# Wider moving operands in the feed-forward units: two activation halves in 512 columns, and 512 weight columns per token-major product

## The reference

```python
x = x + jnp.square(jax.nn.relu(h2 @ w_up)) @ w_down          # layer one, D_FF = 4096
...
# two more layers, each with two gated feed-forwards of width 2816:
# (silu(h @ gate) * (h @ up)) @ w_down, RMS norms before and after
```

## Time and profile before

| what | value |
|---|---|
| median of 3 runs | 1453.48 us (1450.79 to 1454.17) |
| profiled execution, its own time | 1449.68 us |
| its span | 1447.9 us |
| TensorE busy | 1393.1 us, 96% |
| VectorE busy | 915.3 us, 63% |
| ScalarE busy | 723.5 us, 50% |
| GpSimd busy | 192.2 us, 13% |

### The profile page before, as it was taken

The page is one execution under the profiler, slowest core; times in us unless marked ns, Lnnn a source line. Parts: engine busy times, 40 slices in busy tenths (PEclk is TensorE's granted clock), DMA queues, the critical chain, the costliest instruction groups (busy, mean ns, idle before and its releaser), DMA issues.

```text
span 1447.9 us, 28167 instructions
## 1 busy us (share of the span) xinstructions
PE 1393.1 (96%) x11538; PEld 1350.0 (93%) x11538; DVE 915.3 (63%) x1317; ACT 723.5 (50%) x1149; POOL 192.2 (13%) x210
## 2 busy tenths in 40 slices
PE   5889899999999999999999999999999998999998
PEld 5777789999999999998899999999999987999998
DVE  7998776666545655547766565556565467656554
ACT  7722745544434544446447444445454474544443
POOL 0465000022100111004201111011110010111100
PEclk9999899999999999999999999999999999999999
DMA  9233324555554545553434555544555441355551
GB/s 372 102 115 108 139 88 141 186 198 176 202 185 172 198 176 213 179 202 135 158 120 148 189 186 194 199 175 175 185 207 181 169 173 59 120 190 185 194 199 59
DMA packets 36814, 244.33 MB, mean 169 GB/s; under 512 B 4208, under 2 KB 5360, under 8 KB 8816
## 3 DMA queue, kind: packets, MB, share of 16 engines
q1 hardware_dynamic: 34992, 238.17, 45.4%
q10 hardware_dynamic: 1728, 4.81, 0.9%
HBM read 241.67 MB, written 1.05 MB: 168 GB/s over the span
## 4 chain that ended last, share of the span: by engine, by line
PE 84%; DVE 9%; ACT 4%; issue 2%; DMA 1%; DVEq 0%; ACTq 0%
PE ps L1906 50%; PE ps L1948 27%; DVE wlo L1094 3%; PE ps L2144 1%; PE ps L2170 1%; ACT whi L599 1%; PE ps L2160 1%; ACT ahi L853 1%; ACT pP L789 1%; PE ps L1964 1%; PE ps L2049 1%; DVE zz L1279 1%; DVE pP L1385 0%; DVE t L1241 0%; DVE t L1240 0%
## 5 line engine op out<-in xcount | busy, mean ns | idle before, releaser
L1094 DVE TENSOR_TENSOR wlo<-raw,whi 128x1024 fp32r<-128x1024 f32 (+1 forms) x434 | 505.7, 1207 | 256.2 <-ACT whi L599 256.0
L1906 PE MATMUL ps<-ahi,whi 128*128 128x256 f32 x2112 | 598.9, 284 | 21.8 <-DVE wlo L1094 17.5
L599 ACT ACTIVATE whi<-raw 128x1024 fp32r<-128x1024 f32 (+1 forms) x434 | 427.7, 1034 | 348.5 <-PE ps L1948 178.9
L1906 PE MATMUL ps<-alo,whi 128*128 128x256 f32 x2112 | 591.9, 280 | 0.0
L1906 PE MATMUL ps<-ahi,wlo 128*128 128x256 f32 x2112 | 591.1, 280 | 0.0
L1906 PEld LDWEIGHTS ps<-ahi,whi 128*128 128x128 f32 x2112 | 398.6, 189 | 29.1 <-DVE wlo L1094 13.0
L1906 PEld LDWEIGHTS ps<-alo,whi 128*128 128x128 f32 x2112 | 397.9, 188 | 0.7 <-issue 0.7
L1906 PEld LDWEIGHTS ps<-ahi,wlo 128*128 128x128 f32 x2112 | 398.1, 189 | 0.0
L1842 POOL TENSOR_TENSOR hlo<-fh,hhi 128x256 f32 (+3 forms) x104 | 85.8, 825 | 747.4 <-ACT hhi L909 534.5
L1550 DVE TENSOR_TENSOR fa<-ps,r 128x512 f32<-128x512 f32 x104 | 72.0, 692 | 173.8 <-PE ps L1906 173.6
L1948 PE MATMUL ps<-whi,hhi 128*128 128x256 f32 x960 | 149.5, 276 | 0.0
(11 more groups left out here) (350 smaller groups left out, 1346.8 us busy)
## 6 DMA issues: line engine op xcount, KB each, us to landing
raw<-in_w_gu SPq DMA_DIRECT2D x88, 1024.0 KB, 4.8
raw<-in_w_fd SPq DMA_DIRECT2D x44, 1024.0 KB, 4.8
raw<-in_w_up SPq DMA_DIRECT2D x16, 1024.0 KB, 4.8
raw<-in_w_dn SPq DMA_DIRECT2D x16, 1024.0 KB, 4.8
raw<-in_w_ret SPq DMA_DIRECT2D x13, 1024.0 KB, 4.8
raw<-in_w_mg SPq DMA_DIRECT2D x8, 1024.0 KB, 4.9
raw<-in_w_o SPq DMA_DIRECT2D x8, 1024.0 KB, 5.8
raw<-in_w_mem SPq DMA_DIRECT2D x4, 1024.0 KB, 4.8
```

The source lines that it names most:

```text
L599: nc.scalar.activation(whi[:, m % SPL, c], raw[:, n % RAW, c], ACT.Copy).then_inc(S("w_hi"), 1)
L1094: ins = tt(wlo[:, m % SPL, c], raw[:, n % RAW, c], whi[:, m % SPL, c].bitcast(F32), ALU.subtract)
L1906: ins = mm(dst, lhsT, rhs, start=k == 0 and p == 0, stop=k == kt - 1 and p == len(pairs) - 1)
```

## The change

The first pass gets a PE routine of its own, `ffn_unit`. `ahi` and `alo` become two halves of one tile `act2`, and one matmul moves both against `whi` (512 columns, the high products into the left half of a bank, the low ones into the right half); a second matmul of 256 columns adds `wlo` times high to the left half. Each column block now has a bank of its own (banks 0 or 1 and 4 or 5). ACT copies the right half to a new tile `fl`, DVE adds it to the left half and then scales by `r`, once for each column block. ACT's and DVE's orders within a unit change with it. In `down` each stationary block is used against two chunks of 512 weight columns. `hhi` and `hlo` now begin at a multiple of 128 bytes, as the weights do. PE waits ahead of the second token tile of the first down unit, because bank 4 or 5 still holds the last unit's sums. Some semaphores are merged.

```diff
-        w[0] += (64 - w[0]) % 128
+        w[0] += -w[0] % 128
         hhi = sb("hhi", [P, FF1_T, T], F32R, where=w)
...
+        def ffn_banks(g):
+
+            return two(g % 2), two(4 + g % 2)
...
# ScalarE
+                def low_sum(i, u, c):
+                    if c:
+                        sem, v = done(up + u)
+                        act.wait_ge(sem, at_round(v, i, RAW))
+                    else:
+                        act.wait_ge(S("ffn_left"), at_round(h0 + u + 1, i, RAW))
+                    nc.scalar.activation(fl[:, u % 2, c], ffn_banks(g0 + u)[c][:, 1], ACT.Copy).then_inc(S("low_sum"), 1)
...
                 def hidden(i, u):
+                    opening = i is None and u == 0
...
+                        low_sum(i, u, 0)
+                        high(i, u - 1)
+                        weights(up + u, i, UNIT)
+                    if kind == "gu":
+                        act.wait_ge(S("joined"), at_round(3 * (h0 + u) + 2, i, 3 * RAW))
+                        nc.scalar.activation(fs[:, b], fa[:, b, 0:T], ACT.Silu).then_inc(S("silu"), 1)
+                    if not opening:
+                        low_sum(i, u, 1)
...
# VectorE
-                    tt(fab, two((g0 + u) % 2), over(r[:, 0:T], 2), ALU.mult).then_inc(S("evac"), 1)
-                    if i is not None or u:
-                        weights(up + u, i, UNIT)
+                    for c, bank in enumerate(ffn_banks(g0 + u)):
+                        if c and not opening:
+                            weights(up + u, i, UNIT)
+                        dve.wait_ge(S("low_sum"), at_round(2 * (h0 + u) + c + 1, i, 2 * RAW))
+                        tt(fab[:, c], bank[:, 0], fl[:, b, c], ALU.add).then_inc(S("joined"), 1)
+                        dve.wait_ge(S("joined"), at_round(3 * (h0 + u) + 2 * c + 1, i, 3 * RAW))
+                        tt(fab[:, c], fab[:, c], r[:, 0:T], ALU.mult).then_inc(S("evac" if c else "joined"), 1)
...
# TensorE
+            def ffn_unit(n, i=None, need=None, halfway=None):
...
+                for c, bank in enumerate(ffn_banks(g)):
...
+                        ws = slice(k * 2 * P + c * P, k * 2 * P + c * P + P)
+                        mm(bank, whi[:, n_slot(n), ws], act2[:, :, k], start=k == 0, stop=k == KT - 1, skip_group_check=True)
+                        ins = mm(bank[:, 0], wlo[:, n_slot(n), ws], ahi[:, k], start=False, stop=k == KT - 1,
+                                 skip_group_check=True)
+                    ins.then_inc(S("unit_split_done" if c else "ffn_left"), 1)
...
-                                        ws = slice(kk * D + T * c, kk * D + T * c + T)
-                                        ins = mm(two(2 + 2 * t + c // 2)[:, c % 2], x[:, k, xs], wgt[:, n_slot(n), ws],
...
+                                        ws = slice(kk * D + 2 * T * c, kk * D + 2 * T * c + 2 * T)
+                                        ins = mm(PS[2 + 2 * t + c][:, :], x[:, k, xs], wgt[:, n_slot(n), ws],
...
-                     lambda u: pe.wait_ge(S("hid_lo"), h0 + (u + 1) * nup // ndn))
+                     lambda u: pe.wait_ge(S("hid_lo"), h0 + (u + 1) * nup // ndn),
+                     between={(0, 1): lambda: pe.wait_ge(S("evac"), GROUP[dn])})
```

More of the change, by code:

```diff
@@ L914, in hidden @@
                           .then_inc(S("hid_hi"), 1)
+                def hidden(i, u):
+                    opening = i is None and u == 0
+                    b = u % 2
+                    if opening:
+                        weights(up, i, UNIT)
+                        low_sum(i, u, 0)
+                        low_sum(i, u, 1)
+                    else:
+                        low_sum(i, u, 0)
+                        high(i, u - 1)
[4 more added lines that the diff above has]
+                    if not opening:
+                        low_sum(i, u, 1)
                 def result(i, u):
@@ L920, in ffn @@
                 rounds_of(act, nup, hidden, ns)
+                high(None, nup - 1)
                 warm_root()
@@ L1940, in down @@
                         closing = t == 1 and u == n_units - 1
-                        for chunks in ((0, 1), (2, 3)) if closing else (range(4),):
+                        for chunks in ((0,), (1,)) if closing else (range(2),):
                             for kk in range(2):
```

59 lines of the change are left out of this document (31 added, 28 removed).

## The result

The changed kernel takes 1470.09 us (median of 4 runs, 1464.33 to 1473.39) against 1452.87 us of the kernel before beside it: ratio 1.0116, 95% interval 1.0081 to 1.0151. It is slower by 17 us (1.2%), where 34 us less were forecast, and lies outside the range of 1409 to 1450. The profiled execution took 1469.08 us, its span 1467.3, 19.4 more than before.

The account below looks back on a forecast made before the run. PE's matmuls were taken to bound the kernel. Gains of 27.7 (first pass) and 19.4 (down pass), less 1.5, 0.7 and 11.0, made 33.9 us: from 1453.5 to 1420 us, range 1409 to 1450.

Parts of the forecast that it names:

- A 512-column matmul: PE, both passes: one takes 216 ns, the weight load hidden under it; the 256-column one behind it 117.7.
- the bound from above: Highest cost considered for a 512-column matmul, twice a 256-column one: 226.6 ns in the down pass, 235.4 in the first.
- the rival's own break-even: From 226 ns a 512-column matmul on, the change's worth is zero or a loss.
- What a column costs, and what a matmul costs: PE at 2.4 GHz: 256 columns take 106.7 ns, with 11, 6.6 or 13.3 on top; weight load 0.107 us.
- First pass, PE: "gu" units fall from 5.655 to 5.34 us on PE; 88 units gain 27.7 us.
- Down pass: Units take 5.18 us, 0.26 less; with w_out, mhi units and the last w_o, a gain of 19.4 us.
- First pass, ACT and DVE: Their loop takes 5.28 us in "gu", under PE's 5.34, and 5.76 in "up", which costs 0.7 us.
- The wait in front of the down pass: PE stands 1.85 us four times and 3.6 in "up" before the down passes, 11.0 us lost together.
- Opening: At the start of each part unit 2 begins some 0.4 us late, 1.5 us lost.
- Each matmul keeps its excess whatever its width: Rival, both passes: 342 ns a first-pass pair, 226.6 a down matmul; about 1449 us; chance 0.12.
- slower, paid by column: Rival: excess grows by column, equal remainders make a 512-column matmul 240 ns; 1488 us; chance 0.10.

Follow-up runs that it names:

- n: Kernel before with only wlo moved 128 bytes on (ahi and alo, lying behind it, move too): 1442.89 us, one run.
- p: Kernel before with wlo 128 bytes further on for first-pass units than for down units: 1468.25 us, ratio 1.0136.
- b: Down passes given widths of 128 to 448 columns, both operands at multiples of 128 bytes: 111.6 to 202.7 ns a matmul; no total given.
- d_stationary: Changed down products with 64 or 32 stationary tokens, or the moving side 64 bytes on: 230.0 to 231.6 ns at 512 columns, 116.7 and 118.3 at 256.
- f_high_late: Changed kernel with ACT's copy to hhi moved behind the next weights' copy: 1464.28 us, ratio 1.0105.
- e_banks67: Changed kernel with the second block's sums in banks 6 and 7, no wait ahead of the second token tile: 1458.1 us, ratio 1.0061.
- m: As l, with wlo 128 bytes further on and the activations where they were: 1432.3 us, one run.
- l: Kernel before with 512-column down products, whi, wlo, hhi and hlo 64 bytes past a multiple of 128, ahi and alo at one: 1449.12 us, ratio 0.9993.
- g_act0: Changed kernel with act2 alone moved 64 bytes, to a multiple of 128: 1464.29 us.
- h_all: Changed kernel with second sums in banks 6 and 7, ACT's hhi copy later, and act2 at a multiple of 128: 1442.95 us, ratio 0.9955.
- j: Kernel before, addresses only: first-pass whi and wlo 64 bytes past a multiple of 128, ahi and alo at one, hhi at 448 modulo 512: 1439.0 us, ratio 0.9929.

## Why the prediction was wrong, point by point

**"A 512-column matmul"** is the step that failed, and it decides the sign. It was taken as 216 ns "since the excess vanishes in both rows in which the moving side lasts 213 ns". Those rows were of other kinds (plain float32, which passes twice, and half the clock) and did not carry over. Measured: 226.7 to 226.8 in `down`, which is the prediction's own sign of being wrong (0.227 apart), and 233.3 to 233.4 in the first pass and in `w_out`. The excess of 6.6 ns in the down pass did not shrink; it doubled with the width, to 13.3. In the 14 kernels that have them, 512-column matmuls with these operands never followed at under 226 ns over a stretch at full clock, and no pair (346.7 at best) was as short as the three matmuls of 113.4 (340) that 256 columns reach in n. In the down pass the bound from above, 226.6, was the value, in the first pass 235.4 was near the 233.4 measured, and the rival's own break-even, "it decides from 226 ns", told the sign rightly.

The prediction weighed the Trainium skill, TensorE: Matmul & The Clock Gate, section Step-by-step, by which moving operand and weight load are read through ports of their own. Taken strictly, as the prediction took it, placing buffers elsewhere should not change a stream of matmuls, and it does, by up to 6.6 ns in 113.4 (n, p, b): here the measurement decides. It speaks against the strict reading, not for a theft in proportion to the load, since a quarter of the stationary block gave nothing back (d_stationary).

**"What a column costs, and what a matmul costs"**: the pitches (117.8, 113.3, 120) and the load (107; 111.6 in b) held, the conclusion that a delay of the load explains the excess was not: it stays at 320 to 512 columns, where the load has 20 to 100 ns to spare.

**"First pass, PE"**: 27.7 us forecast, 0 measured (353.3 a pair, 5.65 us a unit). The moving side there is two pieces of 1024 bytes, 8192 bytes apart; whether that, beside the addresses, makes its 512 columns dearer than those of `down` was not tried. **"Down pass"**: 19.4 forecast; apart from the stalls 0 in the units with `hhi`, 0.65 lost in `w_out` (233.3 against 2 x 113.3). In the `mhi` units 512 columns went from 240 to 227 ns, as in the rival: 96 x 13.3 ns, 1.3 us where 2.3 were forecast.

**"First pass, ACT and DVE"**: the "gu" loop stayed hidden, as forecast (the parts at 127.7 and 129.5 us as before, waits of 2.0 us in all). The order of its steps can be read in the changed kernel's ACT rows, and ACT waits 0.30 for PE, so PE is the bound:

```profile
512.59 0.42 ACT L918 ACTIVATE hhi<-fh 128x256 f32 x1 [1.72 <-DVE fh L1587]
513.30 2.01 ACT L603 ACTIVATE whi<-raw 128x1024 fp32r<-128x1024 f32 x2 [0.30 <-PE ps L1929]
```

The "up" loop was mis-sized: 5.76 forecast, 6.0 to 6.09 measured, and with it the part at 5.05 us instead of 0.7. The missing 0.33 is DVE's subtraction: 335.98 - 333.33 = 2.65 from start to start where the sum has 2.27, in collision with POOL's, which in the order of before ended 0.4 us ahead of it (329.44 against 329.83). The other terms of the loop come out within 0.03 us. f_high_late shows that this order costs the 5 us; that the collision alone does rests on the rows. The 0.7 itself was a slip: the prediction's own terms give 11 x 0.105 - 5 x 0.315 + 0.4 = 0.0.

**"The wait in front of the down pass"** was right: 1.85 and 3.6 forecast, 11.0 in all; measured 1.67 in a "gu" part, 3.1 in "up", 9.8 in all (with 0.2267 for a matmul its sum gives 4.42 - 2.72 = 1.70):

```profile
608.12 0.73 PE L1995 MATMUL ps<-whi,hhi 128*128 128x512 f32 x2 [1.67 <-DVE fa L1581]
```

e_banks67 took it away, the down passes became 2 us shorter four times and 3.1 once, 11.0 in all, and the ratio fell by 0.0055, 8 us. **"Opening"**: 1.5 forecast, 0 to be seen (the "gu" parts last as before), presumably since a PE that is not faster leaves the two engines their slack; no run took that apart.

**The rivals.** "Each matmul keeps its excess whatever its width" (1449, chance 0.12) was nearest in its mechanism. It gave the first pass 16 us that did not come, since there the excess of the wide matmul is 20, not 11. What happened lies between it and "slower, paid by column" (1488): its formula with the measured 233.4 and 226.7 gives 1.41 x 2.0 + 1.73 x (-0.1) - 13.2 = -10.6 us, 1464; with 353.3 for the pair the first term is 0, -13.4, 1467, and the "up" loop was 4.3 longer than its term. So once the price of the matmul and the "up" loop are put right, the sum comes to 1471, and to 1468 without the opening's 1.5 and with the `mhi` units' 1.3; both are within 2 us of the measured 1470.1.

**What stays open**: what sets the excess. Many of the pitches are multiples of 6.67 ns (16 columns at 2.4 GHz) in these streams of float32r matmuls, and at the half clock nothing is left of it. Addresses modulo 256 take part (m against l, n against before), the widths and the order of operands too, and the same addresses gave 346.7 and 353.3 in two parts of one kernel (g_act0, h_all). A layout with 113.4 in both passes was looked for (p) and not found; the first passes' share of it, 104 x 48 matmuls at 4.4 ns less, is some 21 us, and m has that, with down passes 5 us longer in all.

## What to carry to other kernels

Before merging matmuls to save "the cost of a matmul", measure the merged shape with its own operand format in one stage of the kernel: an excess beyond the columns can grow with the width and cancel the saving, and a price from another format or another clock does not carry over. When a step moves on one engine, look at which operations of DVE and GpSimd now run at the same time, and at which bank is still occupied when the next stage begins: these two cost 11 and 5 of the 17 us. Where PE is bound by a stream of equal matmuls, moving a buffer by 64 or 128 bytes is an edit worth trying, and the width is worth trying again with it: it brought 0.7% here (j), 1.2% together with wide down products (m, one execution), and as easily costs 1.4% (p).

## What the runs showed of the hardware that was not expected

- At full clock a 512-column float32r matmul takes from 226.7 to 233.4 ns, one of 256 columns from 113.3 to 120.0, by where its operands lie; one of 128 columns took 111.6 in both layouts tried. At the half clock 512 columns took 427 and 256 took 213, the columns alone.
- Moving `wlo` by 128 bytes, and `ahi` and `alo` with it, exchanged the pitches of the two passes (117.8 and 113.3 became 113.4 and 117.8); moving `wlo` alone took the first pass from 117.9 to 113.4 (m against l).
- Of two layouts one gave wide down products nothing (226.8 against 2 x 113.3 ns) and the other 8.8 ns each (230.0 against 2 x 119.4).
- With 32 instead of 128 stationary columns a 512-column matmul still took 231.6 ns.
- DVE's and GpSimd's tensor-by-tensor operations lengthen each other when they meet: 2.36 to 2.73 us, 1.30 to 1.87, 0.42 to 1.07.
- One mixer took 92.3 to 92.5 us with the clock at 1.00 and 95.7 to 96.5 in traces in which it stood at 0.50 for 10.2 us of it, whatever the edit.
